# Gate and up of a feed-forward layer as 2x2 block products by Strassen's algorithm, in a float32 transformer kernel on one Trainium2 core

## What is computed

```python
D_FF_2 = 2816
CONV_WIDTH = 3

def conv_ffn(h, w_gate, w_up, conv_w, conv_b, w_down):
    s = h.shape[1]
    g = h @ w_gate
    gp = jnp.pad(g, ((0, 0), (CONV_WIDTH - 1, 0), (0, 0)))
    conv = conv_b
    for j in range(CONV_WIDTH):
        conv = conv + gp[:, j:j + s, :] * conv_w[j]
    return (jax.nn.silu(conv) * (h @ w_up)) @ w_down
...
def second_block(...):
...
        x = x + jnp.concatenate([y_mla, y_diff], axis=-1) @ w_out[i]
        x = x + conv_ffn(rms_norm(x, ffn_norm_g[i]), w_gate[i], w_up[i], conv_w[i], conv_b[i], w_down[i])
        gate = jax.nn.sigmoid(rms_norm(x, ple_norm_g[i]) @ w_ple_gate[i])
        x = x + gate * (p[i] @ w_ple_proj[i])
```

## Time and profile before

| | |
|---|---|
| device time, median of 3 runs | 3087.4 us (3087.19 to 3091.45) |
| span of the profiled execution | 3090.8 us |
| PE busy | 2962.6 us (96%) |
| DVE busy | 1571.1 us (51%) |
| ACT busy | 1017.3 us (33%) |
| chain that ended last, by engine | PE 87%, DVE 8%, ACT 3% |

### The profile page before, as it was taken

How to read it: one execution, slowest core, us unless ns; L and a number is a source line. 1 busy time by engine, 2 the same in 40 slices (tenths; PEclk the granted TensorE clock), 3 DMA queues, 4 the chain that set the end, 5 groups by cost and what they waited for, 6 DMA issues and landing times.

```text
span 3090.8 us, 35157 instructions
## 1 busy us (share of the span) xinstructions
PE 2962.6 (96%) x14780; PEld 2478.1 (80%) x14780; DVE 1571.1 (51%) x1992; ACT 1017.3 (33%) x1375; POOL 104.2 (3%) x60
## 2 busy tenths in 40 slices
PE   8999999998999999999999977889999999999999
PEld 6888878886888888888778756878888888888887
DVE  4257667626444443435641277676435544444464
ACT  3144455534211111113331266766322111112132
POOL 0012210022000000000100000000000000000000
PEclk9999999999999999999999989888999999999999
DMA  4111220122111111111122100000211111111122
GB/s 164 48 35 55 76 96 1 42 96 96 55 49 48 55 48 48 48 48 55 48 84 63 38 8 16 15 1 1 104 40 55 48 44 52 48 50 46 55 82 82
DMA packets 45805, 165.59 MB, mean 54 GB/s; under 512 B 5424, under 2 KB 5936, under 8 KB 45648
## 3 DMA queue, kind: packets, MB, share of 16 engines
q1 hardware_dynamic: 45648, 163.34, 16.2%
HBM read 142.09 MB, written 21.23 MB: 53 GB/s over the span
## 4 chain that ended last, share of the span: by engine, by line
PE 87%; DVE 8%; ACT 3%; issue 2%; DMA 0%; SPq 0%; DVEq 0%; ACTq 0%
PE PS L278 23%; PE PS L280 22%; PE PS L282 22%; PE PS L480 2%; PE PS L482 2%; PE PS L481 2%; PE PS L1181 2%; PE PS L703 2%; PE PS L2682 1%; PE PS L1151 1%; PE PS L1166 1%; DVE H L2354 1%; PE PS L2235 1%; DVE w_lo L272 1%; PE PS L2673 1%
## 5 line engine op out<-in xcount | busy, mean ns | idle before, releaser
L278 PE MATMUL PS<-u_hi_f,w_hi 128*128 128x512 f32 x1408 | 436.0, 391 | 7.1 <-DVE u_lo_f L399 4.7
L280 PE MATMUL PS<-u_lo_f,w_hi 128*128 128x512 f32 x1408 | 434.8, 390 | 0.0
L282 PE MATMUL PS<-u_hi_f,w_lo 128*128 128x512 f32 x1408 | 434.8, 390 | 0.0
L272 DVE TENSOR_TENSOR w_lo<-w_raw,w_hi 128x1024 fp32r<-128x1024 f32 x215 | 268.1, 1255 | 294.0 <-ACT w_hi L266 294.0
L266 ACT ACTIVATE w_hi<-w_raw 128x1024 fp32r<-128x1024 f32 x215 | 225.9, 1053 | 568.1 <-PE PS L282 428.4
L278 PEld LDWEIGHTS PS<-u_hi_f,w_hi 128*128 128x128 f32 x1408 | 264.4, 188 | 65.0 <-issue 7.4
L280 PEld LDWEIGHTS PS<-u_lo_f,w_hi 128*128 128x128 f32 x1408 | 265.1, 188 | 55.4
L282 PEld LDWEIGHTS PS<-u_hi_f,w_lo 128*128 128x128 f32 x1408 | 265.1, 188 | 55.3
L278 PE MATMUL PS<-f_ah,w_hi 128*128 128x512 f32 x640 | 197.0, 389 | 0.0
L280 PE MATMUL PS<-f_al,w_hi 128*128 128x512 f32 x640 | 197.0, 389 | 0.0
L282 PE MATMUL PS<-f_ah,w_lo 128*128 128x512 f32 x640 | 197.0, 389 | 0.0
(11 more groups left out here) (389 smaller groups left out, 5039.8 us busy)
## 6 DMA issues: line engine op xcount, KB each, us to landing
w_raw<-in_weights SPq DMA_DIRECT2D x217, 512.0 KB, 3.6
H<-in_x_t SPq DMA_DIRECT2D x16, 512.0 KB, 3.9
stick_kept<-stick_stage SPq DMA_DIRECT2D x12, 512.0 KB, 2.9
mixer<-stick_kept SPq DMA_DIRECT2D x9, 512.0 KB, 6.8
p_kept<-p_stage SPq DMA_DIRECT2D x8, 512.0 KB, 4.0
h_kept<-H SPq DMA_DIRECT2D x8, 512.0 KB, 5.6
H<-h_kept SPq DMA_DIRECT2D x8, 512.0 KB, 7.4
p_pp<-p_kept SPq DMA_DIRECT2D x8, 512.0 KB, 6.8
```

What stands on the lines that cost most here:

```text
L272: dve.tensor_tensor(self.w_lo[i][:], self.w_raw[i][:], self.w_hi[i][:].bitcast(F32), ALU.subtract).then_inc(*self.s("w_lo").up(g))
L278: ins = e.matmul(banks[i], lh, rh[i], start=first, stop=False)
L280: ins = e.matmul(banks[i], lh, rl[i], start=False, stop=False)
L282: ins = e.matmul(banks[i], ll, rh[i], start=False, stop=last)
```

## The change

In the second feed-forward only (`FAST = (1,)`), gate and up of the tiles 2 to 21 are made together. The weights of a tile are seen as 2x2 blocks: A11 and A12 are the gate's channel tiles 0 to 3 and 4 to 7, A21 and A22 the up's. The activations are 2x2 blocks too: B11 and B12 are channel tiles 0 to 3 for the two halves of the tokens, B21 and B22 channel tiles 4 to 7. Seven block products (`WINO`) take the place of eight. A block product is 4 channel tiles by 512 tokens, 12 matmuls, into one PSUM bank. S1 to S4 are sums of weight blocks, which DVE makes for each tile (`dve_ff_sum`), T1 to T4 sums of activation blocks, which are made once. Three banks are open for a tile (`WINO_BANKS`; x, y and z for places 0, 1 and 2). A product that later ones are added to is first copied out by ACT (`act_ff_copy`), and DVE adds the copies and banks up to gate and up.

The program of this stage is a list of slots (`ff_plan`): 7 products P0 to P6 for a tile, and behind each even tile the 8 output tiles of a down product (`pe_down_slot`), 12 matmuls each. The weight ring is used in halves (`ff_room`): ACT and DVE split a half unit or a sum of 128x512 four slots ahead (`AHEAD`). T1 to T3 are made behind the output projection, T4 when up of tile 1 is done, over a part of `u_hi_f` and `u_lo_f` no longer needed. Weights are packed in another order for this, and a raw unit is held until its last sum is made. The DMA descriptor scratch in SBUF is set to 1024 bytes.

```diff
+WINO = [("A11", "B11", 0), ("S1", "T1", 1), ("S2", "T2", 0), ("A12", "B21", 2), ("S3", "T3", 0), ("S4", "B22", 1),
+        ("A22", "T4", 0)]
+WINO_BANKS = [(0, 1, 2), (3, 4, 6)]
+FAST = (1,)
+AHEAD = 4
...
+            for m, block in enumerate(blocks):
+                step = max(block[2] - AHEAD, blocks[m - 6][3] + 1 if m >= 6 else -1, -1)
+                made.setdefault(step, []).append(m)
...
+    def pe_wino(self, n, x, t, j):
...
+        pe.wait_ge(*self.s("w_lo").at("block", n, m))
+        if opens:
+            self.claim(bank // 2)
+            if t >= 4:
+                pe.wait_ge(*self.s("f_bank_read").at("xyz"[place], n, t - 2))
+        else:
+            pe.wait_ge(*self.s("f_act_made").at(n, t, {2: 0, 4: 2, 5: 1, 6: 4}[j]))
...
+    def act_ff_copy(self, n, x):
...
+        act.wait_ge(*self.s("f_slot").at(n, x))
+        if j == 0:
+            act.wait_ge(*self.ff_raw_free(n, t))
+        if j == 1 and t > 2:
+            act.wait_ge(*self.s("f_up_rows").at("sum", n, t - 1))
+        if j == 4:
+            act.wait_ge(*self.s("f_al").at(n, t - 1))
...
+    def ff_raw_free(self, n, t):
+        if n == 1:
+            return self.s("f_conv").at(t - 1, 1)
...
+    def act_ff_fast(self, n):
...
+        for step in range(N + 1):
+            if step:
+                self.act_ff_copy(n, step - 1)
+            for m in self.made[n].get(step, []):
+                self.act_ff_block(n, m)
+            if step == 0:
+                self.act_ff_late_operands(n)
...
+    def dve_ff_fast(self, n):
...
+                if o == 6:
+                    dve.wait_ge(*self.s("f_slot").at(n, at["P", t, 5]))
+                    dve.wait_ge(*self.s("f_act_made").at(n, t, 2))
+                    dve.tensor_tensor(raw[:, hi], raw[:, hi], self.PS[:, banks[1], :], ALU.add).then_inc(
+                        *self.s("f_bank_read").up("y", n, t))
+                    dve.wait_ge(*self.s("f_bank_read").at("z", n, t))
+                    dve.wait_ge(*self.s("f_bank_read").at("y", n, t))
+                    dve.tensor_tensor((sg, raw)[n][:], raw[:], rows[:], ALU.mult).then_inc(
+                        *self.s("f_gate_rows").up(n, t))
+                if o == 7:
+                    dve.wait_ge(*self.s("f_act_made").at(n, t, 4))
+                    dve.tensor_tensor(prod[:, hi], prod[:, lo], self.part5[:], ALU.add).then_inc(
+                        *self.s("f_up_rows").up("sum", n, t))
+                    dve.wait_ge(*self.s("f_slot").at(n, at["P", t, 6]))
+                    dve.wait_ge(*self.s("f_up_rows").at("sum", n, t))
+                    dve.tensor_tensor(prod[:, lo], self.PS[:, banks[0], :], rows[:, lo], ALU.mult).then_inc(
+                        *self.s("f_bank_read").up("x", n, t))
+                    if n == 1:
+                        self.dve_conv(t, 0)
+                if o == 8:
+                    if n == 1:
+                        self.dve_conv(t, 1)
...
+            for m in self.made[n].get(step, []):
+                self.dve_ff_block(n, m)
+            for m in self.made[n].get(step + 1, []):
+                self.dve_ff_sum(n, m)
...
+    def act_ff_end(self, n, step):
...
+        if c == 0:
+            self.act_split(base + 66)
+        if c == 4:
+            self.act_split(base + 67)
...
+    def act_ff_late_operands(self, n):
+        self.nc.scalar.wait_ge(*self.s("w_used").at(self.ff_units(n)[1][1]))
+        for k in range(4):
+            self.act_ff_high(n, "T4", k)
...
@@ -2804,6 +3315,13 @@
+        for k in range(4):
+            self.dve_ff_raw_operands(1, k)
+            if k:
+                for x in ("T1", "T2", "T3"):
+                    self.dve_ff_low(1, x, k - 1)
```

More of the change, by code:

```diff
@@ new lines, in ff_room, with ff_source @@
+    def ff_room(self, n, m):
+        h = (2 * ((U_FF1, U_FF2)[n] + 4) + m) % 6
+        return h // 2, slice(h % 2 * HALF, (h % 2 + 1) * HALF)
+    def ff_source(self, n, m):
+        gates, ups, downs = self.ff_units(n)
+        name, a, first, last = self.wblocks[n][m]
+        if name in ("S1", "S3"):
+            return None, self.weight_sums[:, 0:HALF]
+        if name in ("S2", "S4"):
+            return None, self.weight_sums[:, HALF:T]
+        if name[0] == "down":
+            g, half = downs[a] + name[1], name[2]
+        else:
+            g, half = (gates if name[1] == "1" else ups)[a], name[2] == "2"
+        return g, self.w_raw[g % RING][:, half * HALF:(half + 1) * HALF]
@@ new lines, in act_ff_block @@
+    def act_ff_block(self, n, m):
+        act, (room, cols), (g, src) = self.nc.scalar, self.ff_room(n, m), self.ff_source(n, m)
+        name, a, first, last = self.wblocks[n][m]
+        if m >= 6:
+            act.wait_ge(*self.s("f_slot").at(n, self.wblocks[n][m - 6][3]))
+        else:
+            base = (U_FF1, U_FF2)[n]
+            act.wait_ge(*self.s("w_used").at(max(g0 for g0 in range(base, base + 4) if g0 % RING == room)))
+        if g is None:
+            act.wait_ge(*self.s("f_made").at(n, a, name))
+        else:
+            act.wait_ge(*self.d(f"w_in{g % RING}").at(g))
+        act.activation(self.w_hi[room][:, cols], src, ACT.Copy).then_inc(*self.s("w_hi").up("block", n, m))
@@ new lines, in act_ff_ah, with dve_ff_al @@
+    def act_ff_ah(self, n, t):
+        act = self.nc.scalar
+        act.wait_ge(*self.s("f_gated").at(n, t))
+        if t >= 2:
+            act.wait_ge(*self.ff_ah_room_free(n, t))
+        else:
+            act.wait_ge(*self.s("f_made").at(n, "T4", 3))
+        act.activation(self.ff_parts(n, t)[0], self.f_prod[n][:], ACT.Copy).then_inc(*self.s("f_ah").up(n, t))
+    def dve_ff_al(self, n, t):
+        dve = self.nc.vector
+        dve.wait_ge(*self.s("f_ah").at(n, t))
+        ah, al = self.ff_parts(n, t)
+        dve.tensor_tensor(al, self.f_prod[n][:], ah.bitcast(F32), ALU.subtract).then_inc(*self.s("f_al").up(n, t))
@@ L1574, in act_ffn @@
             self.act_split(gates[0] + RING)
+        if n in FAST:
+            for m in range(2):
+                self.act_ff_block(n, m)
         self.act_statistics_rows(tag, self.f_rows[n][:])
-        for t in range(FF_TILES):
+        for t in range(2 if n in FAST else FF_TILES):
             if n == 1:
@@ L2913, in small, with ffn_fast @@
         return list(u)
+    def ffn_fast(gate, up, down):
+        u = []
+        for t in range(FF_TILES):
+            u += chan(gate, t * P) + chan(up, t * P)
+            if t >= 2 and t % 2 == 0 and t < FF_TILES - 2:
+                u += rows(down, t - 2) + rows(down, t - 1)
+        for k in range(FF_TILES - 4, FF_TILES):
+            u += rows(down, k)
+        return u
     def ffn(gate, up, down):
```

364 lines of the change are left out of this document (355 added, 9 removed).

## The result

The change makes the kernel faster: 3053.8 us median (3048.86 to 3056.32, four runs) against 3088.2 us for the kernel before beside it, a ratio of 0.9879 with a 95% interval of 0.9866 to 0.9893. The forecast was 3046 us, with a range of 3031 to 3065. The profiled execution is the fastest of the four.

A forecast was written before the change was run, and what follows sets the result against it. The prediction took PE to bound the second feed-forward. Its terms, 54.4 + 0.9 - 10 - 2.4 - 1.8 = 41.1 us, off a median of 3087.4 us gave 3046 us, with a range of 3031 to 3065 us.

The forecast's parts named there:

- What bounds the stage, and the price of a matmul: Second feed-forward: PE alone sets its length; 240 fewer matmuls at 0.2267 us save 54.4 us; the single bank costs nothing.
- Odd tile into even tile: Ahead of P2 at ten boundaries, PE waits 1.0 us for P0's copy, behind the last tap: 10 us lost.
- The start: At P2 of tile 2, PE waits 2.4 us because P0's copy stands behind four T4 parts on ACT.
- The clock: Behind the start's wait a stretch at 1.2 GHz costs 1.8 us once; the ten short waits cost nothing.
- T1 to T3: Behind the output projection, some 18.5 us of DVE work hides in 21.9 us of idle time and costs nothing.
- The end: At the next stage's start, the 0.88 us wait for `w_lo` goes: 0.9 us gained.
- P4 to P6, weights and DMA: Inside the tiles, copies have 1.75 us of room and weight landings about 4 us to spare: no waits.
- The narrower span with the chance of 0.60: Whole kernel: 0.8 to 1.6 us at ten places, 0 to 3.6 for the start's clock: 3038 to 3053 us.
- nobody is late: Rival for the stage: two weight operations slip into gaps, all new waits vanish, 55.3 us saved, 3032 us; chance 0.13.
- The clock falls at the short waits: Rival at the ten short waits: each brings a slow stretch of 1.8 us, giving 3064 us; chance 0.10.
- Late inside every tile: Rival inside the 20 tiles: DVE and ACT late, another 1 us in each, giving 3066 us; chance 0.12.
- slower: Rival at the 80 copies: ACT, held by unmade weight sums, comes 3.3 us late, giving 3170 us; chance 0.04.

The follow-up runs named there:

- fewer: The kernel before with only 240 matmuls left out (channel tiles 5 and 6 of the up product, tiles 2 to 21); 3038.1 us, ratio 0.9822.
- best: The changed kernel with an odd tile's last tap right behind the first, ACT's T4 parts one slot later and `f_ah` of tile 1 later; 3038.2 us, ratio 0.9823.
- taps: The changed kernel with the last convolution tap of an odd tile moved ahead of the weight half and weight sum; 3040.1 us, ratio 0.9834.
- cover: The changed kernel with 28 more chained half-width DVE operations ahead of the T1 to T3 operands; 3063.7 us, ratio 0.9917.
- again: The changed kernel unaltered, run a second time; 3053.4 us, ratio 0.9875 against the kernel before.
- dose3: The changed kernel with three more chained DVE additions for each of 20 tiles ahead of the last tap; 3086.2 us, ratio 0.9979.
- t4: The changed kernel with ACT's four high parts of T4 one slot later, behind the copy of P0; 3051.0 us, ratio 0.9864.
- both: The changed kernel with the last tap right behind the first and ACT's T4 parts one slot later; 3040.0 us, ratio 0.9828.
- dose1: The changed kernel with one more useless DVE addition for each of 20 tiles ahead of the last tap; 3057.0 us, ratio 0.9883.

## Why the prediction was right, point by point

**What bounds the stage, and the price of a matmul**: right. `fewer` measures 54.43 us where 54.4 was worked out. `best` comes within 1.6 us of the same stage, with every product in one bank, so the single bank costs nothing that can be measured.

**Odd tile into even tile**: the mechanism, the place and the number of waits were right, and taps shows it. The size was a little low. From P5's end (2374.51 - 0.20 = 2374.31) to P2 the profile has 9.24 us where the prediction had 9.14, so P2 is 1.08 us late. To this comes 0.08 us between P2's first two matmuls. A wait costs 1.16 us, and ten cost 11.6, not 10. The 0.1 us lies in two DVE operations (P5's bank and the sum for up), each with 0.79 us to the next start where 0.73 was taken. The 0.17 us for release and restart had no row behind it. The profile shows 0.14 from the end of the copy (2382.81 + 0.60) to P2, and the 0.08 behind P2's first matmul. The profile's 0.92 is less than either, since it counts from the modelled end of the matmul before.

**The start**: right in place and cause, with P2 2.03 us late and 0.08 us for the restart, 2.1 us in all for a forecast of 2.4 (its own steps, 2324.6 - 2322.1, give 2.5). On ACT the silu took 0.1 us less and the five operations ahead of the copy 0.25 us less (2317.63 to 2320.23 is 2.60, not 2.85).

**The clock**: it fell once, behind the start, for 3.4 us at 0.50. Eight matmul starts come 0.2 us late, 1.62 us for a forecast of 1.8. That it would not fall behind the ten short waits was right too. That it fell behind the start's wait was in part luck. The forecast took it from one precedent, the 2.39 us wait of the earlier trace rows, and neither that wait nor the start's is followed by a fall in every run. Two windows of 10 us around the end of the wait of the earlier trace rows, first in best, where it was 2.36 us long, then in taps, where it was 2.38 (the last three columns are PEclk, DMA share and GB/s):

```profile
1484.00:1494.00 10.00, 9.98 (x37) 8.09 (x38) 9.97 (x7) 2.13 (x2) 4.01 (x2) 0.83 0.18 54
1480.00:1490.00 10.00, 8.42 (x36) 6.62 (x37) 9.97 (x8) 2.49 (x3) 3.37 (x2) 1.00 0.17 54
```

In best the clock fell (0.83 over the window), in taps it didn't (1.00). The forecast would have been right about this term in four of the six runs that have the start's wait.

The Trainium skill's "TensorE: Matmul & The Clock Gate", section "A second HAM failure mode: psum-queue depth-cycling", tells of a kernel in which frequent small idle gaps between groups of matmuls made the clock swing. With ten gaps, one each 60 us or so, it fell here behind nine when they were 2.88 us long, and behind none at 0.92 or 1.49 us.

**T1 to T3**: right. From the last `f_sums` to tile 2 it is 43.55 us in both kernels, DVE has 3.28 us left where 21.9 - 18.5 = 3.4 was worked out, and cover shows what it would cost without the room.

**The end**: right, the wait is gone. It was worth 1.2 us, not 0.9, since like the others it cost more than the profile shows as idle. **P4 to P6, weights and DMA**: right, no wait for them in the list.

**The sum of the stage**: lost are 11.6 + 2.1 + 1.6 = 15.3 us where the forecast had 14.2. 54.4 - 15.3 = 39.1 against 38.75 measured, and the 0.35 us between them stands in starts that come a little late. With the end, some 40.0 us against a forecast of 41.1. The ratio's interval gives 33 to 41 us.

**The median** is 7.8 us above the forecast, and only 1.1 of this is the sum. Most of the rest is probably the base. Three runs had put the kernel before at 3087.4 us; beside the experiments it was 3092.1, and 3092.1 - 40.0 = 3052.1, near the 3053.4 of again. Beside the result's own runs it was 3088.2, so there the medians lie 34.4 us apart, and the 5.6 us that are missing are within what the runs of one kernel spread. The narrower span with the chance of 0.60, 3038 to 3053 us, does not follow from its terms, which give 3042 to 3054; 3053.8 lies at its upper edge.

The rivals: "nobody is late" fell with the ten waits, though the order of `best` brings it about. "The clock falls at the short waits" did not come true at 0.92 us, but dose3 shows that it would at 2.88 us. "Late inside every tile" and "slower" had no place: no wait stands at P4 to P6 outside t4 and both.

## What to carry to other kernels

When an engine that was half idle is given work that the bound engine needs, average load says little. Follow the one chain in order, start to start, against the slots that the bound engine gives it, and then move whatever nobody needs yet behind what somebody waits for. Here two DVE operations behind the last tap rather than ahead of it were worth 10.9 us, more than a quarter of what the whole change saved in the stage. For an effect of 40 us in 3050, compare the stage by two fixed instructions in both traces; the medians carry several us from elsewhere.

## What the runs showed of the hardware beyond that

**The clock and the length of a wait.** In this stage, where PE was otherwise dense, no wait of 0.9 to 1.5 us was followed by a fall (among them ten each in after, again, t4, dose1 and cover). The start's wait of 1.85 to 1.88 us was followed by one in after, again, dose3 and cover, and by none in taps and dose1, whose program is the same up to there. The wait ahead of 1483.80 is 2.36 to 2.39 us long in all eleven profiles. A fall follows it within 1.6 us in before, after, again, fewer, both and best, and none in taps, t4, dose1, dose3 and cover. At 2.88 us it came nine times in ten. Each fall in the stage lasted about 3.4 us and cost about 1.6. So the length of a wait alone does not decide between 1.85 and 2.9 us; what does stays open.

**Runs of one kernel differ ahead of the stage.** In code that is the same in all, the profiles differ in their stretches below full clock up to 2269 us. One less the granted clock, summed over windows of 10 us, gives 75 us before, 70 after, 77 in again and 60 in cover. This is the likely source of the spread of several us between runs; it was not tested.
